# Last attention of a two-block transformer kernel: memory's heads inside the last queries' product, the compressed branch's first products under selected heads, and a gelu made from exponentials

## The reference, cut to what matters

```python
def compress(u, pos, w1, w2):            # 15 overlapping blocks of 32 tokens, for keys and for values
    ...
    return jax.nn.gelu(flat @ w1) @ w2   # w1 2048x256, w2 256x64
...
q = rmsnorm(q_raw, q_gain) * hd ** -0.5
gates = jax.nn.sigmoid(gate_logits)
# per head: compressed (15 keys), selected and window (both causal over all 256 keys at this length)
return gb[..., 0:1] * o_c + gb[..., 1:2] * o_s + gb[..., 2:3] * o_w
...
y_mem = softmax(q_mem @ mem_k) @ mem_v   # 4 heads, 256 keys, not causal
x = x + concatenate([y_tok, y_mem]) @ w_out
```

## Time and profile before

| | us |
|---|---|
| median of three runs (1566.86 to 1567.7) | 1567.24 |
| the profiled execution | 1565.9 |
| its span | 1564.1 |
| PE busy | 1458.2 (93%) |
| DVE busy | 887.5 (57%) |
| ACT busy | 684.3 (44%) |
| POOL busy | 182.2 (12%) |
| mean granted clock of TensorE | 0.941 |

### The profile page before, as it was taken

The page is one execution under the profiler, slowest core; times in us unless marked ns, Lnnn a source line. Parts: engine busy times, 40 slices in busy tenths (PEclk is TensorE's granted clock), DMA queues, the critical chain, the costliest instruction groups (busy, mean ns, idle before and its releaser), DMA issues.

```text
span 1564.1 us, 24440 instructions
## 1 busy us (share of the span) xinstructions
PE 1458.2 (93%) x10298; PEld 1367.7 (87%) x10298; DVE 887.5 (57%) x1188; ACT 684.3 (44%) x975; POOL 182.2 (12%) x174
## 2 busy tenths in 40 slices
PE   7998999999799899999998959899998888899998
PEld 6997999999799799999976749899998777799997
DVE  5576654555647666545666564454576533565554
ACT  5534544334454453343554423444456422354442
POOL 2002100001200120000122001101023100010000
PEclk9999999999999999999999959999999656899999
DMA  8621365555452137665444602455455400145552
GB/s 230 189 98 58 110 210 189 166 185 166 131 148 95 68 109 230 217 207 165 151 135 141 215 30 88 156 171 206 162 175 156 162 1 0 55 135 183 194 182 88
DMA packets 159657, 225.10 MB, mean 144 GB/s; under 512 B 19081, under 2 KB 127625, under 8 KB 159548
## 3 DMA queue, kind: packets, MB, share of 16 engines
q1 hardware_dynamic: 159548, 223.55, 43.9%
HBM read 222.44 MB, written 1.09 MB: 143 GB/s over the span
## 4 chain that ended last, share of the span: by engine, by line
PE 81%; DVE 11%; issue 3%; ACT 3%; POOL 1%; DMA 0%; DVEq 0%; SPq 0%; ACTq 0%; POOLq 0%
PE ps L2274 16%; PE ps L2276 16%; PE ps L2275 16%; PE ps L2266 4%; PE ps L2267 4%; PE ps L2268 4%; DVE w_lo L1361 2%; PE ps L2920 2%; PE ps L2553 2%; DVE xT L1385 2%; PE ps L2554 2%; PE ps L2555 2%; ACT w_hi L781 1%; DVE h L1400 1%; PE ps L2787 1%
## 5 line engine op out<-in xcount | busy, mean ns | idle before, releaser
L1361 DVE TENSOR_TENSOR w_lo<-raw,w_hi 128x2048 fp32r<-128x2048 f32 (+4 forms) x209 | 478.1, 2293 | 279.9 <-ACT w_hi L781 278.8
L2274 PE MATMUL ps<-xT,w_hi 128*128 128x256 f32 x1600 | 464.4, 290 | 13.4 <-DVE w_lo L1361 6.9
L781 ACT ACTIVATE w_hi<-raw 128x2048 fp32r<-128x2048 f32 (+4 forms) x209 | 392.2, 1879 | 161.3 <-PE ps L2276 79.5
L2275 PE MATMUL ps<-xT,w_hi 128*128 128x256 f32 x1600 | 457.9, 286 | 0.0
L2276 PE MATMUL ps<-xT,w_lo 128*128 128x256 f32 x1600 | 457.8, 286 | 0.0
L2274 PEld LDWEIGHTS ps<-xT,w_hi 128*128 128x128 f32 x1600 | 312.4, 195 | 18.4 <-DVE w_lo L1361 13.5
L2275 PEld LDWEIGHTS ps<-xT,w_hi 128*128 128x128 f32 x1600 | 312.6, 195 | 0.5
L2276 PEld LDWEIGHTS ps<-xT,w_lo 128*128 128x128 f32 x1600 | 312.3, 195 | 0.0
L2274 PE MATMUL ps<-hT,w_hi 128*128 128x256 f32 x640 | 182.7, 285 | 5.4 <-DVE hT L1847 4.6
L2275 PE MATMUL ps<-hT,w_hi 128*128 128x256 f32 x640 | 182.1, 284 | 0.0
L2276 PE MATMUL ps<-hT,w_lo 128*128 128x256 f32 x640 | 182.0, 284 | 0.0
(11 more groups left out here) (320 smaller groups left out, 2100.4 us busy)
## 6 DMA issues: line engine op xcount, KB each, us to landing
raw<-in_w_up_dram SPq DMA_DIRECT2D x54, 1024.0 KB, 5.4
raw<-in_w_down_dram SPq DMA_DIRECT2D x54, 1024.0 KB, 5.0
raw<-in_w_gate_dram SPq DMA_DIRECT2D x22, 1024.0 KB, 5.3
raw<-in_w_in_dram SPq DMA_DIRECT2D x14, 1024.0 KB, 5.4
raw<-in_a_w_in_dram SPq DMA_DIRECT2D x10, 1024.0 KB, 5.3
raw<-in_w_o_dram SPq DMA_DIRECT2D x8, 1024.0 KB, 4.9
raw<-in_w_ple_gate_dram SPq DMA_DIRECT2D x8, 1024.0 KB, 4.9
raw<-in_w_out_dram SPq DMA_DIRECT2D x8, 1024.0 KB, 4.9
```

Of the source, the lines that this page charges most:

```text
L781: nc.scalar.activation(w_hi[:, p % RH, 0:piece_width(p)], raw[:, p % RR, 0:piece_width(p)], ACT.Copy).then_inc(E["hi_ready"], 1)
L1361: nc.vector.tensor_tensor(w_lo[:, p % RH, 0:w], raw[:, p % RR, 0:w], w_hi[:, p % RH, 0:w].bitcast(F32), ALU.subtract).then_inc(E["lo_ready ...
L2274: nc.tensor.matmul(out_, w[0][:, kk, c], x(0, k), start=start and j == 0, stop=False, skip_group_check=True)
L2275: nc.tensor.matmul(out_, w[0][:, kk, c], x(1, k), start=False, stop=False, skip_group_check=True)
```

## The change

`query_units(2)` (memory's queries turned) moves into the first query product. The scores of memory's heads 0 and 1 are issued before the last product, and their transposes, values and the scores of heads 2 to 4 between its slices; their scores use two banks. The hidden products move from before the heads to steps 4 to 7, half a matrix a step, and what follows in the compressed branch moves to steps 9 to 19. Output rows start at step 20, with 5 to 8 units a step. On DVE `move_pT(i)` comes directly behind `logits(i + 1)`; groups are gathered one step earlier, behind it. The gates become 1/(1 + exp(-x)), with the reciprocal on DVE. The gelu becomes h/(1 + exp(-2ch(1 + 0.044715 h^2))): Copy and Square on ACT, a polynomial with a lower bound on DVE, Exp on ACT, and 1 +, reciprocal and multiply on DVE over 30x512.

```diff
+q8F = q8.rearrange("p b s -> p (b s)")
+hfun = tflat[0:NSA_G * NCMP, 768:768 + 2 * CMP_HID].rearrange("p (w n) -> p w n", w=2)
...
-        src = PS[T % 4][0:self.w, 0:len(self.srcs) * S].rearrange("p (b s) -> p b s", s=S)
+        src = self.place(T)[0:self.w, 0:len(self.srcs) * S].rearrange("p (b s) -> p b s", s=S)
...
-    return plain(z1, 512 * c, 4 - 2 * c, q8[:, 4 * c:4 + 2 * c, :], COLS[("b_q_gain_2", 0)])
+    return plain(z1, 512 * c, 4 - 2 * c, q8[:, 4 * c:4 + 2 * c, :], COLS[("b_q_gain_2", 0)], (4, 7)[c])
...
-BESIDE_2 = ((0, 0, 4), (0, 4, 7), (0, 7, 10), (0, 10, 13), (0, 13, 16),
-            (1, 0, 4), (1, 4, 7), (1, 7, 10), (1, 10, 13), (1, 13, 16), (2, 0, 4), (2, 4, 8), (2, 8, 12), (2, 12, 16))
+ROWS_2 = 20
+BESIDE_2 = ((0, 0, 6), (0, 6, 11), (0, 11, 16), (1, 0, 6), (1, 6, 11), (1, 11, 16), (2, 0, 8), (2, 8, 16))
...
+def scores_bank(i):
+    return PS[i % 2 if i < MEM_H else 0]
...
+GROUP_OUT = (1, 2, 3, 4, 8, 9, 10)
+COMP_OUT = (5, 6, 7)
...
```

ACT's loop over the heads:

```diff
-        ahead(ACT.Sigmoid)
+        ahead(ACT.Exp)
         evac_units(kv_units())
+        evac_units(query_units(2))
         wide_evac(("q", 0), 512, z1[:, :, 0:512], ("mix", 1))
-        head_squares([(PbF, z1[:, :, 0:512])])
...
+        def hidden_units(w):
+            act.wait_ge(E["piece_used"], FIRST[("cmp", w)] + 2)
+            act.wait_ge(E["zeroed"], 1)
+            src = PS[(1, 6)[w]][0:NSA_G * NCMP, 0:CMP_HID]
+            nc.scalar.activation(act_hid[0:NSA_G * NCMP, w, :], src, ACT.Copy)
+            nc.scalar.activation(hfun[:, w, :], src, ACT.Square).then_inc(E["gel_sq"], 1)
...
             exps(i)
+            if i == 0:
+                act.wait_ge(E["flat_ready"], 1)
+                for w in range(2):
+                    nc.scalar.activation(flatR[0][w], flat[:, w].rearrange("p l g c -> p (l g c)"), ACT.Copy
+                                         ).then_inc(E["fhi"], 1)
             if i == 1:
+                used(("q", 1), 0)
+            if i == 2:
+                evac_units(query_units(0))
+            if i == 3:
+                wide_evac(("q", 1), m0 - 512, z1[:, :, 512:m0], ("mix", 1))
+                head_squares([(q8F[:, 1024:1536], z1[:, :, 512:NSA_H * HD])])
+                nc.scalar.activation(gate[:, :, :], z1[:, :, NSA_H * HD:m0], ACT.Exp, scale=-1.0
+                                     ).then_inc(E["gat_e"], 1)
+            if i == 4:
+                used(("cmp", 0), 0)
+            if i == 5:
+                hidden_units(0)
+                used(("cmp", 0), 1)
+            if i == 6:
+                evac_units(query_units(1))
+                used(("cmp", 1), 0)
+            if i == 7:
+                hidden_units(1)
                 used(("cmp", 1), 1)
-            if i == 6:
+            if i == 8:
+                act.wait_ge(E["gel_u"], 1)
+                nc.scalar.activation(hfun, hfun, ACT.Exp, scale=-2 * (2 / np.pi) ** 0.5 * 0.044715
+                                     ).then_inc(E["gel_e"], 1)
...
+            if i == 12:
                 rounded_pair(6)
-            if i == 7:
+            if i == 15:
...
-            if i == 9:
+            if i == 16:
                 for t in range(NT):
...
             if i == 22:
                 rounded_pair(2)
-            if i == 24:
+                used(("w_out", 1), 0)
+            if i == 25:
                 used(("w_out", 1), 1)
...
```

DVE's:

```diff
+        def factors_of_gates():
+            dve.wait_ge(E["gat_e"], 1)
+            link(nc.vector.tensor_scalar(gate[:, :, :], gate[:, :, :], 1.0, None, ALU.add))
+            nc.vector.reciprocal(gate[:, :, :], gate[:, :, :]).then_inc(E["gat_done"], 1)
...
         logits(0)
         for i in range(NL):
             if i + 1 < NL:
                 logits(i + 1)
+            move_pT(i)
+            if i == 0:
+                dve.wait_ge(E["zsq"], 3)
+                head_sums(16, 16, q8F[:, 0:1024])
+                for w in range(2):
+                    dve.wait_ge(E["fhi"], w + 1)
+                    nc.vector.tensor_tensor(flatR[1][w], flat[:, w].rearrange("p l g c -> p (l g c)"),
+                                            flatR[0][w].bitcast(F32), ALU.subtract).then_inc(E["flo"], 1)
+            if i == 1:
+                dve.wait_ge(E["hn_r"], 5)
+                scaled(16, 8, 0)
+                used(("q", 1), 0)
             if i == 2:
+                evac_units(query_units(0))
+            if i == 3:
+                m0 = B_IN - MEM_W
+                wide_evac(("q", 1), m0 - 512, z1[:, :, 512:m0], ("mix", 1))
+            if i == 4:
+                dve.wait_ge(E["zsq"], 4)
+                head_sums(0, 8, q8F[:, 1024:1536])
+                used(("cmp", 0), 0)
+                group(0)
+            if i == 5:
+                dve.wait_ge(E["hn_r"], 6)
+                scaled(0, 4, 512)
+                factors_of_gates()
+                used(("cmp", 0), 1)
+            if i == 6:
+                evac_units(query_units(1))
+                used(("cmp", 1), 0)
+            if i == 7:
+                dve.wait_ge(E["gel_sq"], 2)
+                link(nc.vector.scalar_tensor_tensor(hfun, hfun, 1 / 0.044715, act_hid[0:NSA_G * NCMP, :, :],
+                                                    op0=ALU.add, op1=ALU.mult))
+                nc.vector.tensor_scalar(hfun, hfun, -1120.0, None, ALU.max).then_inc(E["gel_u"], 1)
+                used(("cmp", 1), 1)
+            if i == 8:
+                dve.wait_ge(E["gel_e"], 1)
...
```

```diff
+                link(nc.vector.tensor_scalar(hfun, hfun, 1.0, None, ALU.add))
+                link(nc.vector.reciprocal(hfun, hfun))
+                hid2 = act_hid[0:NSA_G * NCMP, :, :]
+                nc.vector.tensor_tensor(hid2, hid2, hfun, ALU.mult).then_inc(E["gel_done"], 1)
+                dve.wait_ge(E["gat_done"], 1)
+            if i == 11:
                 dve.wait_ge(E["kc_mm"], 1)
                 nc.vector.tensor_copy(kvc, PS[6][:, 0:4 * HD].rearrange("p (a d) -> p a d", a=4)
                                       ).then_inc(E["kvc_ready"], 1)
...
-                dve.wait_ge(E["gat_done"], 1)
-            if i in (11, 12, 13):
-                compressed_out(4 * (i - 11))
-            if i in (9, 13, 17, 21, 25):
+            if i in (8, 12, 16, 20, 24):
                 group(i // 4 - 1)
-            if i == 16:
+            if i in (17, 18, 19):
+                compressed_out(4 * (i - 17))
+            if i == 19:
                 rest_pair(0)
-            if i == 19:
-                used(("w_out", 1), 0)
             if i == 22:
                 rest_pair(2)
-            if i == 24:
+                used(("w_out", 1), 0)
+            if i == 25:
...
```

PE's:

```diff
                 pe.wait_ge(E["kd_ready"], 2)
                 units(kv_units())
+            if k == 6:
+                pe.wait_ge(E["qn_ready"], 2)
+                units(query_units(2))
         wide_product(("q", 0), 512, ("mix", 1), fresh=False, between_=between_)
-        wide_product(("q", 1), B_IN - MEM_W - 512, ("mix", 1), fresh=False)
-        pe.wait_ge(E["qn_ready"], 2)
-        units(query_units(2))
...
-        hidden_rows(0)
-        pe.wait_ge(E["qn_ready"], 3)
-        units(query_units(0))
...
         def scores(i):
             job, J = jobs[i], J0 + i
-            if i and not jobs[i - 1].causal:
-                pe.wait_ge(E["e_done"], NT * J)
-            else:
+            if 2 <= i <= MEM_H:
+                pe.wait_ge(E["e_done"], NT * (J - 1))
+            elif i > MEM_H:
                 pe.wait_ge(E["l_done"], NT * J)
...
                 pe.wait_ge(E["rep_done"], 1)
                 for w in range(2):
...
                             m = nc.tensor.matmul(PS[6][:, (2 * w + g) * HD:(2 * w + g + 1) * HD], gel4[:, w, j, g, :],
                                                  w2[:, w, j, :], start=j == 0, stop=j == 1)
                 m.then_inc(E["kc_mm"], 1)
-            if i == 4:
+            if i == 13:
                 pe.wait_ge(E["kcd_ready"], 1)
                 for g in range(NSA_G):
                     m = nc.tensor.transpose(PS[7][:, 16 * g:16 * g + 16], kcd[0:16, g, :], ident[0:16, 0:16])
                 m.then_inc(E["kct_mm"], 1)
-            if i == 5:
+            if i == 14:
                 pe.wait_ge(E["kct_ready"], 1)
                 for t in range(NT):
                     for a in range(0, NSA_H, 2):
...
                         m = nc.tensor.matmul(PS[4][:, c:c + 32], q8[:, a // 2, t * P:t * P + P],
...
+        def between_(k):
+            if k % 2:
+                transposes(k // 2)
+                if k > 1:
+                    values(k // 2 - 1)
+            if k in (1, 3):
+                scores(k // 2 + 2)
+            if k == 5:
+                pe.wait_ge(E["qn_ready"], 3)
+                pe.wait_ge(E["wide_a"], n["wide"])
+                pe.wait_ge(E["wide_d"], n["wide"])
+                units(query_units(0))
+            if k == 6:
+                units_moved()
+                scores(MEM_H)
+        units_moved()
         scores(0)
-        gelu_turned(1)
```

(23 more changed lines are left out.)

202 lines of the change are left out of this document (80 added, 122 removed).

## The result

| | before | changed |
|---|---|---|
| median, us | 1567.05 (1564.49 to 1567.7, 4 runs) | 1541.18 (1535.45 to 1542.98, 4 runs) |
| profiled execution, us | 1565.9 | 1535.45 |
| its span, us | 1564.1 | 1533.6 |

The ratio is 0.9832, with a 95% interval of 0.9802 to 0.9862: 25.9 us faster. I had forecast 1554.3, 12.9 us faster, and a range from 1547 to 1563.

What follows compares the result with a forecast made beforehand. Bound first by waits over DVE, POOL and ACT, then by PE at half clock. The touched stretch's parts, 47.5 + 67.7 + 34.6 = 149.8 against 162.7, save 12.9 us: 1554.3 us, range 1547 to 1563.

Steps and rivals of the forecast that it cites:

- Part A: Touched stretch from its start to the scores of head 9: 73.6 us before, forecast 47.5, 26 less.
- 3 for the low clock: Up to the scores of head 9: 3 us allowed for two stretches in which PE's clock drops.
- handovers: Up to the scores of head 9: 2.5 us added for PE and DVE handing work to each other every head.
- The moved query units' wait: Up to the scores of head 9: PE idles 2 us more, for the split behind the scaling.
- Rival 1: Steps 0 to 8: DVE's queue holds up heads more than allowed; gain only 5.7 us, time 1561.5; chance 0.17.
- Part B: From the scores of head 9 to those of head 21: 60.7 us before, forecast 67.7, 7 more.
- The wait behind the long reciprocal: Gelu's 30x512 reciprocal on DVE takes 3.4 us; PE idles 3.6 us behind it and the work queued after.
- rival 3: Clock rises between the scores of heads 9 and 21 as gaps close; saves 23.5 us, time 1531; chance 0.05.
- Part C: From the scores of head 21 to the last values: forecast 34.6 us, 6.2 more, including 2.1 for low clock.
- waits for groups: Values waiting for DVE to gather four heads, 5.1 us over four waits, go because the copy now comes first.
- two of three table loads: Up to the scores of head 9: two ACT table loads of 1.28 us each were counted as gone.

Runs made afterwards that it cites:

- a_whole: The changed kernel with the last queries' product made in one piece and memory's steps behind it; 1543.4 us, 20.6 us faster than the kernel before.
- a_cover9: The changed kernel with gelu by ACT's function, last turned blocks ahead of the split, another split moved to head 11, nine transposes in step 9; gain 38.3 us.
- a_again: The changed kernel, nothing altered, timed again; 1541.93 us, ratio 0.9848 to the kernel before.

## Why the prediction was right or wrong

**Part A: right, 3.8 us too long.** I had placed the work at 42 us and added 3 for the low clock and 2.5 for handovers. PE idled 3.8 us for memory's first exponentials (forecast 2.9) and nowhere else for long; the clock was low once, for 6.8 us. Steps 4 to 7 took 4.9, 4.9, 5.4 and 4.7, as placed. The handovers cost nothing: PE was busy for 19.7 of 19.9 us beside a DVE that was busy for 16.5. The moved query units' wait of 2 us did not come. Rival 1 (DVE takes PE's place) is out: DVE had only 3.4 us to spare in these four steps, and PE did not see it. Of the 29.9 us by which A shrank, the slices of the product account for 3.0 (a_whole); no run takes back the move of the hidden products under the heads, so what that move gives is not shown by an edit.

**Part B: the step that failed.** "Twelve steps (8 to 19) now have no output rows, so I take them at 0.50": that was 43.0, with the compressed branch at 19.8, all at the low clock. In the profile the first 3.8 us and the last 10.1 us of the part ran at 1.00. They held 2.1 and 9.1 us of PE's work, 11.2 us that would have been twice as long at the low level: 58.2 + 11.2 = 69.4, against my 67.7. So the count of work was good to 2 us, and the clock alone was wrong. In the two profiles where it rose 3.4 us before the end of the part, B was 62.1, with 2.1 and 3.4 us of work at 1.00: 67.6 by the same count. The wait behind the long reciprocal was 3.2 us (forecast 3.6), its length 3.34 (forecast 3.4 by the slope of the earlier trace rows). The estimate of 5.5 us that I had worked out from the repeat count in the Trainium skill (VectorE: DVE Perf Modes, "First, the fixed hardware budget") does not agree with this trace; the measurement decides. One step earlier PE idled 1.6 and 0.8 us (forecast 1.3).

**The level, where I argued from the wrong row.** From 1257 to 1277 PE showed busy throughout and stayed at 0.50, and from this I took a busy PE to be no reason for a rise. But PE at the low clock is busy with the same work for twice as long: at full clock those steps would hold 2.0 us of work each. What such a stretch shows is that the clock doesn't come back by bare heads; it does not show that they bring it down. a_cover9 had one at 1.00, in 1.9 us, and kept that level until PE idled. I gave rival 3, a rise in B, 0.05, and had priced it from step 10 on (1531). What came was its half, from step 17 on in half of the profiles. The Trainium skill's sentence (TensorE: Matmul & The Clock Gate, "What's actually happening") that activity releases the throttle fits these runs. Its "Part 4: PE-mode transpose", by which transposes don't count as busy in the same way, does not, if it means transposes such as these, which the profile shows as MATMUL rows: six or nine extra ones a step brought the clock back as nine extra products did.

**Part C: right.** 33.6 against 34.6; the low stretch that I had allowed for did not come.

**The sum.** Of the 14.3 us between 149.8 and 135.5, 9.5 are B's, 3.8 A's and 1.0 C's. My range allowed for a low stretch more or less in A and C, and for none less in B. That is what made it too narrow: 0.05 for all cases in which the clock rises, in a stretch where I had priced it at 23.5 us. Against the profile of a_again, which is nearer to a median, the three parts are short by 5.6 (B), 3.6 (A) and 1.0: B is the largest miss there too, though not by much.

**The DVE order was undervalued.** I named the waits for groups as going, as one item of B. Alone in the kernel before it is worth 12.6 us, half as much as the change: 6.6 us of waits in part B, and then the clock behind them.

**The exponentials were not a gain.** I booked "two of three table loads" with A and the reciprocal with B, and did not ask what one pair of loads at the right place costs. It is 5.7 us cheaper in the medians, and 1.7 to 5.6 us in part B by where the clock rises.

## What to carry to other kernels

A stretch at the low clock is a price of its own: sum PE's work in both levels, and let the range reach to the other one, even when a row shows PE busy at the low level, since there "busy" counts the slow duration. A gap of a microsecond or two on PE is to be priced with what the clock does behind it: 1.2 us of useless work that filled one was worth 3 us of part B in the profiles (52.3 to 49.3), though the gains of the two kernels, 37.4 and 38.3 us, don't tell them apart. Work that keeps PE from idling and the clock from falling is worth a trial, and so is a second profile of the same kernel, since the clock can rise at another step there. Before an expensive function is rebuilt from cheaper ones, gather its uses at one place and count what one switch costs there.
